# Products of two rotation-table steps on ScalarE, and the tables' steps in other chunks of the FFN

## The chip, the core and the metric

The kernel runs on one core of a Trainium2 chip. A core has TensorE for matrix products, VectorE, ScalarE and GpSimd for the rest, and SyncE, which here only issues DMAs. The metric is the device time of one execution in microseconds, lower is better. One execution is also profiled; its trace gives every instruction's start and duration, counted from the span's start.

## The reference, cut to what matters

Two layers, each with three sub-layers: an FFN, a mixer of four token mixers side by side, a second FFN. The change touches what is done during the first FFN of each layer for the fourth mixer, the S5.

```
for l in range(DEPTH):
    y = _swiglu(u, ffn_w13[l, 0], ffn_w2[l, 0])      # silu(u @ w1) * (u @ w3), then @ w2
    x = _layer_norm(ALPHA * x + 0.5 * gate[:, 0] * y, ...)
    y = _hybrid_mixer(u, ...)                        # A, B, C and S5
    ...
# S5: a diagonal complex recurrence over 256 positions
mag = jnp.exp(lr * dt)
a_re, a_im = mag * jnp.cos(li * dt), mag * jnp.sin(li * dt)
# s[t] = a * s[t - 1] + bu[t], y = Re(C s) + D u
```

All is float32. The sizes: 256 tokens, model width 1024, FFN width 2816.

## The kernel before, in words

**The recurrence by rotation.** The kernel turns the inputs `bu` by the angle of each position, so that a real scan with the factor `rho` is left, and turns the result back. For that it needs cos and sin of n times the angle for n = 0 to 128: `cos_t` and `sin_t`, 128 partitions x 8 tiles x 129. They are built by doubling in seven steps, k = 0 to 6, with m = `TABLE_STEPS[k]` = 1, 2, 4 up to 64. Step k knows the entries 1 to m and makes m + 1 to 2m with the addition theorem: four products into four pieces of `rot_flat` (`t4[0]` to `t4[3]`), a difference and a sum. In `table_ops` VectorE makes each product in one instruction over all 8 tiles (L1245), then the difference (L1248) and the sum (L1251). The semaphore `rot_step` counts all six; a step's sums wait for 4 counts beyond the step before. `TABLE_AT` says behind which chunk of the first FFN which steps are made; SyncE waits once for all of them (chunk 9 of layer 0, as it loads new data into `rot_flat`), and VectorE before the mixer.

**An FFN chunk.** The FFN's 2816 columns are done in 11 chunks of 256, each of two tiles of 128 (ft = 0, 1). The products run in fp32r, and each operand is split into a high and a low part, so that three matmuls make one product of nearly full precision. Per chunk, the engines do, each in the written order:
- TensorE (`ffn_chunk`, L547 to L549): 96 matmuls of the input weights, tile 0 and then tile 1; in some chunks then a sum or a spread of modulation (L521, L530: `spread_gate`); then 24 matmuls with the output weights (L573, L576, L577), the first half with `h` of tile 0, the second with that of tile 1 (in the last chunk all of token tile 0 comes first).
- ScalarE: silu of tile 0 (L1658), the high part of the next chunk's input weights, tile 0 (`w_in_hi`, L1665), the same for tile 1, a gate copy in some chunks, and then `w_out_high` (L1673), two instructions. These wait until TensorE has done the whole chunk, as there is one pair of `w_out_hi` buffers.
- VectorE: the low part of the output weights, twice (`w_out_low`, L1057); then for each tile `ffn_tile`: silu times the linear half (L1041), the high part (L1044) and the low part (L1046) of `h` into `h_parts`; behind it the low part of the next chunk's input weights (L1052). Then, if the chunk stands in `ADA`, one block of the adaLN projection (`ada_block`, L974 or L977 and seven of L980, 128x512 each). Behind these come the small S5 jobs at their chunk: `residual`, `s5_angles`, `s5_poles`, the table steps, `s5_inverse`, `s5_gains`, and `c_blocks` (L1227) and `b_blocks`, which prepare the matrices C and B of the S5.
- SyncE issues the loads of the next chunk's weights, each when the ring's buffer is free, and the block of the adaLN projection.

In layer 0 every chunk of the first FFN has an `ADA` block but the last (which has one in two halves), in layer 1 chunks 0 to 4 and 7 to 9. Chunks 7 and 8 of layer 0 and 3 and 4 of layer 1 spread a gate. The queues are written out by hand; the order in each engine's queue is that of the code.

Of the kernel before, what the change touches and what calls it, by code (L numbers as in the profile page):

```python
# [22 lines left out]
ACT = mybir.ActivationFunctionType  # L23
# [68 lines left out]
TABLE_STEPS = (1, 2, 4, 8, 16, 32, 64)  # L92
ROT_STEPS = 6 * len(TABLE_STEPS)
# [7 lines left out]
def trunk(nc, x, c, ada_w, ada_b, ln_g, ln_b, ffn_w13, ffn_w2, w_in, w_out, sinks, w_uq, w_iq,  # L101
# [3 lines left out]
    with ctx:  # L105
        def sb(name, shape, dt=F32):
            offset[name] = (nc.sbuf_base + 31) // 32 * 32
            return ctx.enter_context(nc.sbuf_tensor(name, shape, dt))
# [7 lines left out]
        def sem(name):  # L116
            if name not in sems:
                sems[name] = ctx.enter_context(nc.semaphore(name))
            return sems[name]
# [28 lines left out]
        cos_t = sb("cos_t", [P, 8, HT + 1])  # L148
        sin_t = sb("sin_t", [P, 8, HT + 1])
# [38 lines left out]
        rot_flat = sb("rot_flat", [P, 8 * T])  # L188
# [42 lines left out]
        def heads(ap):  # L231
            return ap.rearrange("p (t h) -> p t h", t=2)
# [25 lines left out]
        def ff_group(f, c):  # L258

            return (0, G_FFN2)[f] + c  # L260
# [643 lines left out]
        def _(v):  # L904
# [155 lines left out]
            def ffn_chunk(l, f, c):  # L1060

                slot = ff_group(f, c) % 2
                tile = ff_tile(l, f, c)
                for ft in range(2):
                    w_out_low(slot, ft, tile + ft)
                for ft in range(2):
                    ffn_tile(ft, tile)
                    if c != CHUNKS - 1:
                        w_in_low(1 - slot, ft, tile + (2 + ft))
                if c in ADA[l, f]:  # L1070
                    n = ADA[l, f][c]
                    ada_block(n, ada_w_sb, "ada_loaded", n + 1 if n < 10 else n - 1)
# [45 lines left out]
            def residual(l, s, k):  # L1118

                n, tt = l * 3 + s, k // 2  # L1120
                if k % 2 == 0:
                    v.wait_ge(sem("ln_bc_loaded"), (n + 1) * 32)
                    v.wait_ge(sem("xn_act"), n * 2 + (tt + 1))
                    if tt == 1:
                        v.wait_ge(sem("xn_dve"), n + 1)
                    v.tensor_tensor(x_sb[:, tt, :], xn[:, tt, :], ln_bc[:, 0, :], ALU.mult).then_inc(sem("x_step"), 1)
                else:
                    v.wait_ge(sem("x_step"), n * 2 + (tt + 1))
                    v.tensor_tensor(x_sb[:, tt, :], x_sb[:, tt, :], ln_bc[:, 1, :], ALU.add).then_inc(sem("x_ready"), 1)
# [19 lines left out]
            for l in range(DEPTH):  # L1149
# [4 lines left out]
                def s5(ins):  # L1154

                    ins.then_inc(sem("s5_step"), 1)
                    step[0] += 1
                    v.wait_ge(sem("s5_step"), l * STEPS + step[0])
# [17 lines left out]
                def s5_poles():  # L1176

                    v.wait_ge(sem("sin_ready"), l + 1)
                    s5(v.tensor_tensor(S5["sh2"], S5["sinh"], S5["sinh"], ALU.mult))
                    s5(v.tensor_scalar(S5["cos"], S5["sh2"], -2.0, 1.0, ALU.mult, ALU.add))  # L1180

                    v.tensor_copy(cos_t[:, :, 1:2], S5["cos"].unsqueeze(2)).then_inc(sem("rot_start"), 1)
                    v.tensor_copy(sin_t[:, :, 1:2], S5["sin"].unsqueeze(2)).then_inc(sem("rot_start"), 1)
                    s5(v.tensor_tensor(S5["a_re"], S5["rho"], S5["cos"], ALU.mult))
                    s5(v.tensor_tensor(S5["a_im"], S5["rho"], S5["sin"], ALU.mult))
                    s5(v.tensor_scalar(S5["am1"], S5["a_re"], 1.0, None, ALU.subtract))
# [10 lines left out]
                def s5_gains():  # L1197

                    s5(v.tensor_tensor(S5["k1"], S5["k1"], S5["k2"], ALU.add))
                    s5(v.tensor_tensor(S5["k_re"], S5["k1"], S5["rden"], ALU.mult))  # L1200
                    s5(v.tensor_tensor(S5["k3"], S5["a_im"], lr, ALU.mult))
                    s5(v.tensor_tensor(S5["k4"], S5["am1"], li, ALU.mult))
                    s5(v.tensor_tensor(S5["k3"], S5["k3"], S5["k4"], ALU.subtract))
                    s5(v.tensor_tensor(S5["k_im"], S5["k3"], S5["rden"], ALU.mult))
# [18 lines left out]
                def c_blocks():  # L1223

                    v.wait_ge(sem("params_loaded"), (l + 1) * 16 * PARAM_DMAS)
                    for k, sign in ((0, 1.0), (1, -1.0)):
                        v.scalar_tensor_tensor(c_blk[:, k, :, :], c_blk[:, k, :, :], sign,  # L1227
                                               block_mask[:, :].unsqueeze(1).to_broadcast([P, 2, P]), ALU.mult, ALU.mult
                                               ).then_inc(sem("c_blk_ready"), 1)

                def table_ops(k, ops):
# [8 lines left out]
                    for op in ops:  # L1240
# [8 lines left out]
                        else:  # L1249
                            v.wait_ge(sem("rot_step"), at + 4)  # L1250
                            v.tensor_tensor(sin_t[:, :, hi], t4[2], t4[3], ALU.add).then_inc(sem("rot_step"), 1)  # L1251

                TABLE_AT = {3: ((0, range(6)), (1, range(6))), 4: ((2, range(6)), (3, range(6))), 5: ((4, range(6)),),
                            6: ((5, range(6)),), 7: ((6, range(0, 3)),), 8: ((6, range(3, 6)),)}

                for c in range(CHUNKS - 1):
                    ffn_chunk(l, 0, c)
                    if l and c < 4:
                        residual(l - 1, 2, c)
                    if c == 3:  # L1260
                        s5_poles()
                    for k, ops in TABLE_AT.get(c, ()):
                        table_ops(k, ops)
                    if c == 4:
                        s5_inverse()
                    if c == 5:
                        s5_gains()
                    if c == 9:
                        c_blocks()
                        b_blocks()  # L1270
                    if c == 0 and l == 0:
                        bias_constants()
                    if c == 1:
                        v.wait_ge(sem("prm_turned"), l + 1)
                        v.tensor_copy(prm[:, :], PS[:, 7, 0:ROWS]).then_inc(sem("prm_ready"), 1)
                    if c == 2:
                        s5_angles()
# [106 lines left out]
                for tt, cols in ((0, slice(0, P)), (1, slice(P, 384))):  # L1384
                    v.wait_ge(sem("z_read"), l * NZ + 1 + ZN[("t0", "t1")[tt]])
                    for h in range(H):
                        w = tokv[:, tt, 192 + h:193 + h]
                        src = work[0][:, h, cols]
# [97 lines left out]
                for h in range(H):  # L1486
                    g = PS[:, 6 + h // 2, (h % 2) * T:(h % 2 + 1) * T]
                    v.scalar_tensor_tensor(work[0][:, h, 0:T], g, heads(rcol)[:, 0, h:h + 1], mask_c[:, :], ALU.add, ALU.add)
                    ins = v.scalar_tensor_tensor(work[0][:, h, T:384], g[:, P:T], heads(rcol)[:, 1, h:h + 1], mask_c[:, 0:P],
                                                 ALU.add, ALU.add)  # L1490
# [130 lines left out]
        def _(a):  # L1621
# [26 lines left out]
            def copy_gate(n):  # L1648
# [3 lines left out]
                a.activation(gate_bc[s % 2][:, hf * 512:(hf + 1) * 512], PS[:, 7, :], ACT.Copy, scale=1.0 if s % 3 == 1 else 0.5  # L1652
                             ).then_inc(sem("gate_ready"), 1)

            def silu_tile(ft, tile):
                a.wait_ge(sem("ag_ready"), tile + (ft + 3))
                a.wait_ge(sem("h_done"), tile + (ft + 1))
                a.activation(silu_ring[:, ft, :], PS[:, 4 + ft, 0:T], ACT.Silu).then_inc(sem("silu_ready"), 1)  # L1658
# [16 lines left out]
            def ffn_chunk(l, f, c):  # L1675

                last = c == CHUNKS - 1
                slot = ff_group(f, c) % 2
                tile = ff_tile(l, f, c)
                for ft in range(2):  # L1680
                    silu_tile(ft, tile)
                    if not last:
                        if ft == 0:
                            a.wait_ge(sem(f"w_in_loaded{1 - slot}"), in_loads(l, ff_group(f, c + 1)))
                        w_in_high(1 - slot, ft, tile + (2 + ft))
                if not last:
                    if c - 1 in ADA[l, f] and gate_of(ADA[l, f][c - 1]) is not None:
                        copy_gate(ADA[l, f][c - 1])
                    w_out_high(l, f, c + 1)
                elif c - 1 in ADA[l, f] and gate_of(ADA[l, f][c - 1]) is not None:  # L1690
                    copy_gate(ADA[l, f][c - 1])
# [4 lines left out]
            for l in range(DEPTH):  # L1696
                w_out_high(l, 0, 0)
                for c in range(CHUNKS):
                    ffn_chunk(l, 0, c)
                    if c == 1:  # L1700
                        a.wait_ge(sem("prm_ready"), l + 1)
                        a.activation(S5["dt"], log_dt[:, :], ACT.Exp).then_inc(sem("dt_ready"), 1)
                    if c == 2:
                        a.wait_ge(sem("lrdt_ready"), l + 1)
                        a.activation(S5["rho"], S5["lrdt"], ACT.Exp)
                        a.wait_ge(sem("angle_ready"), l + 1)
                        a.activation(S5["sin"], S5["r0"], ACT.Sin)
                        a.activation(S5["sinh"], S5["r0"], ACT.Sin, scale=0.5).then_inc(sem("sin_ready"), 1)
# [245 lines left out]
```

## Time and profile before

| | |
|---|---|
| median of 3 runs | 1121.68 us (1121.27 to 1126.46) |
| profiled execution | 1123.7 us, its span 1121.4 us |
| TensorE busy | 1054.8 us, 94% |
| VectorE busy | 903.8 us, 81% |
| ScalarE busy | 422.4 us, 38% |
| GpSimd busy | 38.9 us, 3% |
| TensorE's granted clock, mean | 0.971 of full speed |
| HBM, mean | 223 GB/s |

The busy shares are means over the whole span. Durations of neighbouring instructions on one engine overlap by a little, so the time that one costs in a row is the distance of two starts. The granted clock is the share of full speed that TensorE got.

### The profile page before, as it was taken

The page shows a single profiled execution, that of the slowest core. Times are in us where ns is not written, and L with a number is a line of the kernel's source. Part 1 is how long each engine was busy: PE and PEld are TensorE (multiplying, and loading weights), DVE is VectorE, ACT ScalarE, POOL GpSimd, SP SyncE. Part 2 cuts the span into 40 slices and gives each one's busy share as a digit, 9 for nine tenths or more (in the row PEclk, how much of TensorE's full clock was granted, in tenths as well). Part 3 has the DMA queues.
Part 4 walks back from the last instruction along what each step waited for, and adds up shares of the span by engine and source line. Part 5 has one row for each costly group of instructions (what it writes and reads, how often), then busy time and mean ns, then how long its engine had stood idle before and what let it go on. Part 6 is the DMA issues. An engine that isn't in the chain of part 4 may idle for free.

```text
span 1121.4 us, 16954 instructions
## 1 busy us (share of the span) xinstructions
PE 1054.8 (94%) x6865; PEld 929.0 (83%) x6865; DVE 903.8 (81%) x1499; ACT 422.4 (38%) x566; POOL 38.9 (3%) x56
## 2 busy tenths in 40 slices
PE   1899999989999899999999999999999989999994
PEld 1899989977865799999989989998787569999994
DVE  6798999989975798988877998798797578755555
ACT  0445334312462334333333443332236333333331
POOL 1000000003000100000000000000300010000000
PEclk9999999989999899999979999999999989999998
DMA  9899998972351588898955886887225156564540
GB/s 367 277 327 310 345 306 301 313 217 75 95 188 38 188 296 288 308 325 286 338 189 190 302 303 196 287 317 199 78 89 203 55 188 233 181 220 148 196 151 37
DMA packets 184504, 250.82 MB, mean 224 GB/s; under 512 B 25372, under 2 KB 133216, under 8 KB 183404
## 3 DMA queue, kind: packets, MB, share of 16 engines
q1 hardware_dynamic: 184428, 249.76, 65.2%
q8 instruction: 54, 0.88, 0.3%
q14 instruction: 22, 0.18, 0.0%
HBM read 248.69 MB, written 1.05 MB: 223 GB/s over the span
## 4 chain that ended last, share of the span: by engine, by line
PE 79%; DVE 14%; issue 2%; ACT 2%; DMA 2%; SPq 0%; POOL 0%; POOLq 0%; DVEq 0%; ACTq 0%
PE PS L547 13%; PE PS L548 13%; PE PS L549 13%; PE PS L654 8%; PE PS L573 6%; PE PS L577 6%; PE PS L576 6%; PE PS L879 2%; DVE w_in_lo L1052 2%; PE PS L661 2%; PE PS L739 2%; DVE acc L980 2%; DMA xn<-in_ada_w_dram 2%; DVE qk_tanh L980 1%; DVE w_out_lo L1057 1%
## 5 line engine op out<-in xcount | busy, mean ns | idle before, releaser
L547 PE MATMUL PS<-u_hi,w_in_hi 128*128 128x256 f32 x1408 | 399.8, 284 | 7.2 <-DVE u_lo L1011 4.4
L549 PE MATMUL PS<-u_hi,w_in_lo 128*128 128x256 f32 x1408 | 400.1, 284 | 0.0
L548 PE MATMUL PS<-u_lo,w_in_hi 128*128 128x256 f32 x1408 | 399.3, 284 | 0.0
L547 PEld LDWEIGHTS PS<-u_hi,w_in_hi 128*128 128x128 f32 x1408 | 270.6, 192 | 10.2 <-issue 5.5
L548 PEld LDWEIGHTS PS<-u_lo,w_in_hi 128*128 128x128 f32 x1408 | 269.3, 191 | 1.6
L549 PEld LDWEIGHTS PS<-u_hi,w_in_lo 128*128 128x128 f32 x1408 | 268.7, 191 | 0.0
L1052 DVE TENSOR_TENSOR w_in_lo<-w_in_ring,w_in_hi 128x2048 fp32r<-128x2048 f32 x88 | 201.5, 2289 | 31.8 <-ACT w_in_hi L1665 31.6
L1665 ACT ACTIVATE w_in_hi<-w_in_ring 128x2048 fp32r<-128x2048 f32 x88 | 168.1, 1914 | 1.3 <-DMA w_in_ring<-in_ffn_w_dram 1.3
L573 PE MATMUL PS<-w_out_hi,h_parts 128*128 128x512 f32 x352 | 144.8, 411 | 7.1 <-DVE h_parts L1046 7.1
L1658 ACT ACTIVATE arena<-PS 128x256 f32<-128x256 f32 x88 | 33.9, 385 | 301.3 <-PE PS L549 301.2
L1673 ACT ACTIVATE w_out_hi<-w_out_ring 128x1024 fp32r<-128x1024 f32 x88 | 88.6, 1055 | 146.4 <-PE PS L577 146.4
L577 PE MATMUL PS<-w_out_hi,h_parts 128*128 128x512 f32 x352 | 139.0, 395 | 0.0
L576 PE MATMUL PS<-w_out_lo,h_parts 128*128 128x512 f32 x352 | 138.6, 394 | 0.0
L1057 DVE TENSOR_TENSOR w_out_lo<-w_out_ring,w_out_hi 128x1024 fp32r<-128x1024 f32 x88 | 103.7, 1219 | 16.3 <-ACT w_out_hi L1673 16.0
L654 PE MATMUL PS<-uT,w_in_ring 128*128 128x256 f32 (+1 forms) x416 | 95.4, 386 | 3.6 <-ACT uT L1634 2.5
L1041 DVE TENSOR_TENSOR arena<-arena,PS 128x256 f32<-128x256 f32 x88 | 36.8, 419 | 75.6 <-ACT arena L1658 75.5
L654 PEld LDWEIGHTS PS<-uT,w_in_ring 128*128 128x128 f32 (+1 forms) x416 | 77.9, 190 | 18.8 <-issue 4.5
L573 PEld LDWEIGHTS PS<-w_out_hi,h_parts 128*128 128x128 f32 x352 | 66.5, 189 | 27.8 <-issue 15.0
L980 DVE SCALAR_TENSOR_TENSOR acc<-arena,cs,acc 128x512 f32<-128x512 f32 x112 | 84.2, 752 | 4.0
L576 PEld LDWEIGHTS PS<-w_out_lo,h_parts 128*128 128x128 f32 x352 | 66.5, 189 | 15.8 <-issue 2.6
L577 PEld LDWEIGHTS PS<-w_out_hi,h_parts 128*128 128x128 f32 x352 | 66.4, 189 | 15.8
L1910 POOL TENSOR_TENSOR rstd<-var_eps,neg_half 128x1 f32<-128x1 f32 x12 | 10.5, 875 | 888.0 <-DVE var_eps L1106 888.0
(302 smaller groups left out, 1068.6 us busy)
## 6 DMA issues: line engine op xcount, KB each, us to landing
w_in_ring<-in_ffn_w_dram SPq DMA_DIRECT2D x88, 1024.0 KB, 7.7
arena<-in_ada_w_dram SPq DMA_DIRECT2D x30, 2048.0 KB, 8.5
w_out_ring<-in_ffn_w_dram SPq DMA_DIRECT2D x44, 1024.0 KB, 6.6
w_in_ring<-in_w_in_dram SPq DMA_DIRECT2D x6, 1024.0 KB, 6.8
w_in_ring<-in_w_in_dram SPq DMA_DIRECT2D x10, 512.0 KB, 4.9
w_out_ring<-in_w_out_dram SPq DMA_DIRECT2D x4, 1024.0 KB, 9.7
w_in_ring<-in_w_in_dram SPq DMA_DIRECT2D x2, 2048.0 KB, 9.4
w_in_ring<-in_w_out_dram SPq DMA_DIRECT2D x4, 1024.0 KB, 6.2
```

The lines of the kernel that those rows point to most:

```text
L547: pe.matmul(y, hi, u_hi[:, kt, :], start=(i == 0), stop=False)
L548: pe.matmul(y, hi, u_lo[:, kt, :], start=False, stop=False)
L549: mm = pe.matmul(y, lo[:, kt, half, :], u_hi[:, kt, :], start=False, stop=(i == KT - 1))
L573: mm = pe.matmul(y, h_hi, w_out_hi[ft][:, cols], start=(first and ft == 0), stop=False)
L576: pe.matmul(y, h_hi, w_out_lo[slot][:, ft, cols], start=False, stop=False)
L577: mm = pe.matmul(y, h_lo, w_out_hi[ft][:, cols], start=False, stop=(last and ft == 1))
L654: mm = pe.matmul(o[0:w, :], w_in_ring[(G_MIX + m) % 2][:, kt, c0:c0 + w], uT[:, kt, :], start=(kt == 0), stop=(kt == KT - 1))
L980: v.scalar_tensor_tensor(acc[:, :], part(buf, t), cs[:, t:t + 1], acc[:, :], ALU.mult, ALU.add).then_inc(sem("acc_step"), 1)
L1052: v.tensor_tensor(w_in_tile(w_in_lo, slot, ft), w_in_tile(w_in_ring, slot, ft), w_in_hi[ft][:, :, :, :].bitcast(F32), ALU.subtract).then_i ...
L1057: v.tensor_tensor(w_out_lo[slot][:, ft, :], w_out_ring[slot][:, ft, :], w_out_hi[ft][:, :].bitcast(F32), ALU.subtract).then_inc(sem("w_out ...
L1665: a.activation(w_in_hi[ft][:, :, :, :], w_in_tile(w_in_ring, slot, ft), ACT.Copy).then_inc(sem("w_in_high"), 1)
L1673: a.activation(w_out_hi[ft][:, :], w_out_ring[slot][:, ft, :], ACT.Copy).then_inc(sem("w_out_high"), 1)
```

## The change

Three edits. First, in steps 5 and 6 of the tables ScalarE makes the products: a new function `table_products` with 8 instructions for each of the four products, one for each tile, as ScalarE takes its factor as one value for each partition; 32 a step. It stands behind ScalarE's chunk 6 and 7 in layer 0, and 7 and 8 in layer 1. VectorE makes only the ops 4 and 5 (difference and sum) of these steps, behind the chunks of the same numbers. Second, `TABLE_AT` now differs by layer: in layer 0 steps 0 to 4 stay where they were; in layer 1 steps 0 to 3 come behind chunk 5 and step 4 behind chunk 6. Third, `c_blocks` comes behind chunk 8 in layer 0, and stays behind chunk 9 in layer 1.

```
-                TABLE_AT = {3: ((0, range(6)), (1, range(6))), 4: ((2, range(6)), (3, range(6))), 5: ((4, range(6)),),
-                            6: ((5, range(6)),), 7: ((6, range(0, 3)),), 8: ((6, range(3, 6)),)}
+                steps = lambda *ks: tuple((k, range(6)) for k in ks)
+                TABLE_AT = ({3: steps(0, 1), 4: steps(2, 3), 5: steps(4), 6: ((5, (4, 5)),), 7: ((6, (4, 5)),)},
+                            {5: steps(0, 1, 2, 3), 6: steps(4), 7: ((5, (4, 5)),), 8: ((6, (4, 5)),)})[l]
...
+                    if c == 8 + l:
+                        c_blocks()
                     if c == 9:
-                        c_blocks()
                         b_blocks()
...
+            def table_products(l, k):
+
+                m = TABLE_STEPS[k]
+                t4 = [rot_flat[:, 512 * q:512 * q + 8 * m].rearrange("p (i n) -> p i n", i=8) for q in range(4)]
+                a.wait_ge(sem("rot_step"), l * ROT_STEPS + 6 * k)
+                for q, (src, by) in enumerate(((cos_t, cos_t), (sin_t, sin_t), (sin_t, cos_t), (cos_t, sin_t))):
+                    for i in range(8):
+                        ins = a.activation(t4[q][:, i, :], src[:, i, 1:1 + m], ACT.Copy, scale=by[:, i, m:m + 1])
+                    ins.then_inc(sem("rot_step"), 1)
...
                 for c in range(CHUNKS):
                     ffn_chunk(l, 0, c)
+                    if c in (6 + l, 7 + l):
+                        table_products(l, c - l - 1)
```

## Rows read from the trace of the kernel before

**Rows 1.** Waits of TensorE, 105 to 240 us: total, times, longest.

```profile
PE PS L573 <- DVE h_parts L1046: 4.4, 6, 2.5
```

**Rows 2.** Timeline of TensorE, layer 0: start us, us, engine, line, tiles.

```profile
162.65 0.28 PE L547 MATMUL PS<-u_hi,w_in_hi 128*128 128x256 f32 x1
...
174.00 1.02 PE L530 MATMUL PS<-acc,ones 128*128 128x512 f32 x2
...
233.21 0.47 PE L573 MATMUL PS<-w_out_hi,h_parts 128*128 128x512 f32 x1 [2.51 <-DVE h_parts L1046]
```

**Rows 3.** Timeline of ScalarE, layer 1, `w_out_hi` of chunks 4 to 7.

```profile
655.72 2.01 ACT L1673 ACTIVATE w_out_hi<-w_out_ring 128x1024 fp32r<-128x1024 f32 x2 [4.13 <-PE PS L577]
...
674.58 2.02 ACT L1673 ACTIVATE w_out_hi<-w_out_ring 128x1024 fp32r<-128x1024 f32 x2 [4.88 <-PE PS L577]
...
692.51 2.02 ACT L1673 ACTIVATE w_out_hi<-w_out_ring 128x1024 fp32r<-128x1024 f32 x2 [4.44 <-PE PS L577]
...
709.41 2.02 ACT L1673 ACTIVATE w_out_hi<-w_out_ring 128x1024 fp32r<-128x1024 f32 x2 [3.41 <-PE PS L577]
```

**Rows 4.** Timeline of ScalarE, layer 0, chunk 7 and the start of chunk 8.

```profile
162.91 2.01 ACT L1673 ACTIVATE w_out_hi<-w_out_ring 128x1024 fp32r<-128x1024 f32 x2 [3.90 <-PE PS L577]
168.53 0.39 ACT L1658 ACTIVATE arena<-PS 128x256 f32<-128x256 f32 x1 [3.61 <-PE PS L549]
...
180.67 2.02 ACT L1673 ACTIVATE w_out_hi<-w_out_ring 128x1024 fp32r<-128x1024 f32 x2 [3.79 <-PE PS L577]
```

**Rows 5.** Timeline of VectorE, layer 0, chunks 6 to 10.

```profile
169.41 0.43 DVE L1248 TENSOR_TENSOR cos_t<-rot_flat 128x256 f32<-128x256 f32 x1
...
170.08 2.35 DVE L1057 TENSOR_TENSOR w_out_lo<-w_out_ring,w_out_hi 128x1024 fp32r<-128x1024 f32 x2
172.36 0.41 DVE L1041 TENSOR_TENSOR arena<-arena,PS 128x256 f32<-128x256 f32 x1
...
175.68 0.41 DVE L1041 TENSOR_TENSOR arena<-arena,PS 128x256 f32<-128x256 f32 x1
...
185.18 0.69 DVE L1245 TENSOR_TENSOR rot_flat<-cos_t 128x512 f32<-128x512 f32 x1
...
203.01 0.69 DVE L1248 TENSOR_TENSOR cos_t<-rot_flat 128x512 f32<-128x512 f32 x1
...
204.22 2.36 DVE L1057 TENSOR_TENSOR w_out_lo<-w_out_ring,w_out_hi 128x1024 fp32r<-128x1024 f32 x2
...
220.05 0.75 DVE L1227 SCALAR_TENSOR_TENSOR c_blk<-c_blk,block_mask 128x256 f32<-128x256 f32 x2
...
231.87 0.41 DVE L1041 TENSOR_TENSOR arena<-arena,PS 128x256 f32<-128x256 f32 x1
```

**Rows 6.** ScalarE: timeline rows, and two groups by shape (busy us, mean ns).

```profile
98.88 0.21 ACT L1707 ACTIVATE s5p<-s5p 128x8 f32<-128x8 f32 x1
99.00 0.19 ACT L1708 ACTIVATE s5p<-s5p 128x8 f32<-128x8 f32 x1
...
309.42 2.88 ACT L1754 ACTIVATE work_flat<-work_flat,small 128x128 f32<-128x128 f32 x8
...
L1754 ACT ACTIVATE work_flat<-work_flat,small 128x256 f32<-128x256 f32 x16 | 6.8, 493 | 0.0
...
L1754 ACT ACTIVATE work_flat<-work_flat,small 128x128 f32<-128x128 f32 x16 | 5.1, 391 | 2.2 <-DVE small L1501 2.1
```

**Rows 7.** Timeline of VectorE, layer 1, chunks 3 to 5.

```profile
663.06 0.17 DVE L1245 TENSOR_TENSOR rot_flat<-cos_t 128x8 f32<-128x8 f32 x1
...
664.52 2.35 DVE L1057 TENSOR_TENSOR w_out_lo<-w_out_ring,w_out_hi 128x1024 fp32r<-128x1024 f32 x2
...
670.11 0.41 DVE L1041 TENSOR_TENSOR arena<-arena,PS 128x256 f32<-128x256 f32 x1
...
688.04 0.41 DVE L1041 TENSOR_TENSOR arena<-arena,PS 128x256 f32<-128x256 f32 x1
```

**Rows 8.** Busy time by window, 232 to 240 us; PEclk is the granted clock.

```profile
232.00:240.00 8.00, 6.53 (x24) 5.04 (x24) 6.54 (x16) 0.00 (x0) 0.56 (x1) 0.79 0.96 199
```

## The prediction, made before the changed kernel was run

> **What bounds the kernel now.** I read the busy shares first (in the table above): TensorE 94%, VectorE 81%, ScalarE 38%. A share is an average, so I looked next at TensorE's waits over the chunks of layer 0's first FFN [rows 1]: 4.4 us in 135 us, all of it for `h_parts`, which VectorE writes. TensorE sets the pace, and VectorE is only just in time. The timelines then give the rhythm of a chunk. I count from T, the chunk's first matmul.
>
> TensorE does the input products until T + 11.35 (162.65 to 174.00 [rows 2]) and then the output products. An undisturbed chunk is 16.90 long (692.51 to 709.41 [rows 3]), so the output products take 5.55, in two halves of 2.78: the first needs `h` of tile 0, the second, due at T + 14.13, that of tile 1. Chunks that also spread a gate take 17.76 (162.91 to 180.67 [rows 4]); there the second half is due at 17.76 - 2.78 = T + 14.98.
>
> ScalarE makes `w_out_hi` at T + 0.26, two instructions in 2.01, and has nothing more to do until the first silu, at T + 5.88 (168.53 [rows 4]).
>
> VectorE runs, in this order: table work, `w_out_low` twice, the multiply of tile 0, `w_in_low`, the multiply of tile 1. In chunk 7 of layer 0 the reader sees 170.08, 172.36 and 175.68 [rows 5]: 2.28 from `w_out_low` to the first multiply (m0), 3.32 from there to the second (m1). TensorE starts on an `h` 1.34 after its multiply (231.87 [rows 5], 233.21 [rows 2]). So VectorE may start `w_out_low` at 14.13 - 1.34 - 3.32 - 2.28 = T + 7.19 before an undisturbed chunk gets longer, and at T + 8.04 in a chunk with a gate. Chunk 7 started it at T + 7.43. There is little to spend.
>
> **Part 1: VectorE gives up eight products in each layer, and waits instead.** In place of four products with two sums, VectorE makes two sums. The sums of step 5 take 0.67 (169.41 to 170.08), those of step 6 take 1.21 (203.01 to 204.22); four products of step 5, of the sums' shape, took about 4 x 0.34 = 1.36 [rows 5]. But the sums wait until ScalarE has made all four groups, 32 instructions, and ScalarE begins these only behind `w_out_hi` of the next chunk. Queued behind the waiting sums on VectorE are the next chunk's `w_out_low` and both multiplies, and TensorE waits for these.
>
> The trace has no ScalarE instruction of 32 or 64 columns with a scale taken from a column. The nearest: `over_sums` (L1754), the same Copy with such a scale from SBUF to SBUF. It takes 391 ns for 128 columns and 493 ns for 256, and four of each end 2.88 us after the first starts [rows 6]. The durations add up to 3.54, so consecutive ones overlap by 0.66/7 = 0.094. The slope is 0.102/128 = 0.80 ns a column. That makes 0.314 for 32 columns and 0.340 for 64, and a step from one to the next of 0.22 and 0.245. I take these. The lower end is the shortest start-to-start step of two small instructions there, 0.12 at 8 columns (98.88 to 99.00 [rows 6]), without such a scale: with 24 and 56 columns more, 0.14 and 0.165.
>
> The products start at T + 0.26 + 2.01 - 0.09 = T + 2.18.
> Step 5: the last ends at 2.18 + 31 x 0.22 + 0.31 = T + 9.31. Sums from T + 9.34, `w_out_low` at T + 10.01, m0 at 12.29, TensorE's output products at 13.63 (due 11.35), m1 at 15.61, second half at 16.95, chunk ends at T + 19.73.
> Step 6: the last ends at 2.18 + 31 x 0.245 + 0.34 = T + 10.12. Sums, `w_out_low` at 11.36, m0 13.64, TensorE at 14.98, m1 16.96, second half at 18.30, end at T + 21.08.
>
> VectorE itself would be ready for step 5's sums at about T + 5.4 (169.41 less 1.36, less 162.65), and for step 6's at 15.61 + 9.50 (175.68 to 185.18 [rows 5]) - 19.73 = T + 5.4, so ScalarE's end decides both. ScalarE's silu comes 3.4 to 4.3 late; with `w_in_hi` behind it, it has caught up by about T + 12, long before VectorE asks at m1.
>
> The price, chunk by chunk (the sums of layer 0 fall at the start of chunks 7 and 8, both with a gate; those of layer 1 at the start of 8 and 9, both undisturbed, as their `ADA` entries hold no gate):
> layer 0: 19.73 - 17.76 = +1.97, and 21.08 - 17.76 = +3.32;
> layer 1: 19.73 - 16.90 = +2.83, and 21.08 - 16.90 = +4.18.
> Together +12.30. The lateness does not run on: after chunk 8 VectorE comes to `w_out_low` of chunk 9 at 16.96 + 9.50 - 21.08 + 0.67 (the c blocks) = T + 6.05.
>
> **Part 2: `c_blocks` of layer 0 moves from chunk 9 to chunk 8.** Two instructions, 0.75 [rows 5], 0.67 when the overlap with the next is taken off. At its old place it lies in an unbroken run of VectorE before the last chunk's multiplies, for which TensorE waits 2.51 [rows 2]: -0.67. At its new place there is room (T + 6.05 against 8.04): 0. In layer 1 it stays.
>
> **Part 3: layer 1's steps 0 to 4 go to chunks 5 and 6.** Chunks 4 and 5 of layer 1 are long: 655.72 to 674.58 is 18.86, and 17.93 follow to 692.51 [rows 3]. Steps 0 and 1 took 1.46 (663.06 to 664.52 [rows 7]). Without them m1 of chunk 4 (670.11) comes at 668.65 and TensorE can use it at 669.99, T + 14.53 < 14.98: chunk 4 takes 17.76, -1.10. Without steps 2 and 3 as well, another 1.46 at least, m1 of chunk 5 (688.04) could come at 685.12, T + 11.9 of a chunk that starts at 673.22; TensorE uses it by T + 13.3 < 14.13: 16.90, -1.03. At the new places VectorE is free: chunks 5 and 6 of layer 1 have no ada block (8 x about 0.76). Should that cover be missing, the 3.3 us of steps 0 to 3 would show in full. DMA issues don't move, and SyncE's one wait on the tables (`rot_step`, chunk 9) is met earlier.
>
> **Sum:** +12.30 - 0.67 - 2.13 = +9.5 us. The profiled execution took 1123.7 (span 1121.4 and 2.3 around it), so it would be 1133.2. The median of the runs shown is 1121.68, 2.0 below that execution; I predict it at 1131.2.
>
> **Rules of the Trainium skill weighed.** The trace has four products on VectorE in about 1.4 us [rows 5] and, by the step worked out above, 32 instructions in 7 us on ScalarE. The Trainium skill (ScalarE: Activation LUTs, section Rules for kernel authors) says to use VectorE and not ScalarE for multiplications. The trace agrees; by that rule the +12.30 would not be there, and the sum would be -2.8. The same table budgets about 0.3 us for each ACTIVATE and 0.83 ns an element. The trace contradicts that as a step: [rows 6] have eight in 2.88 us, where that budget makes 3.7.
>
> **Rivals.**
> *A, ScalarE in time, no change.* The small products run at the lower end's step, and ScalarE's idle stretch of 3.6 us before the first silu nearly holds them. Step 5 then ends at 6.71 and costs +0.22 in layer 1, nothing in layer 0; step 6 ends at 7.55, `w_out_low` 8.79, second half 15.73, +0.75 and +1.60. Sum 2.57 - 2.80 = -0.2: 1121.4. It decides at a step of 0.131, below which step 5 costs nothing. For it: that row of 8 columns. Against it: the closer form has the scale operand, and its fixed part (391 - 102 - 94 = 0.195 us) is paid by each.
> *B, faster.* If the products ended before VectorE was ready at T + 5.4, only parts 2 and 3 would remain, and step 5's relief: 1121.68 - 2.8 = 1118.9. This needs a step of 0.10, under any row. VectorE's high share speaks for it; that TensorE waits so little [rows 1] caps what relief can give.
> *C, slower still: the clock falls.* After the wait of 2.51 at the end of layer 0 the granted clock was 0.79 over 8 us [rows 8]: 1.7 us of full speed lost, part of it at 1.2 GHz. The new waits are 2.3 us (step 5) and 3.6 us (step 6, less in layer 0, where the gate fills 0.86). 0.5 us before the second half absorbs some; a fall costs 1.2. One or two are likely and stand against my slightly high step; all four make +4.8: 1136.
> *D, no overlap at all.* If each small instruction cost what its duration says, without the overlap of 0.094, each of the four stages would end 31 x 0.094 = 2.9 later: +11.7, 1142.9. The row of eight speaks against it. By the Trainium skill's budget (above) it would be 3.3 each, near 1144.6.
>
> **Chances.** Forecast 0.64; A, or something between A and the forecast, 0.18 (of which half under 1127.3); B 0.02; C 0.13; D 0.03. The likeliest case by itself runs from 1127.5 (a step of 0.19) to 1134 (two falls of the clock). Range 1123 to 1137: it leaves out most of A's own point, B and D. A measurement of this kernel can tell about 0.5%, 5.6 us: faster than 1116.1 0.02; within 0.14; slower than 1127.3 0.84.
>
> **What would show it.** In layer 0's chunks 7 and 8: silu 0 at about T + 9.3 and 10.1 in place of 5.88; VectorE idle about 4 and 5 us before its two sums, released by ScalarE; chunk lengths 19.7 and 21.1. In layer 1: chunks 4 and 5 at 17.8 and 16.9, chunks 8 and 9 at 19.7 and 21.1. The last chunk's wait of 2.51 unchanged, with everything behind 0.67 nearer to the chunk's start. Wrong would be: a step of ScalarE's products under 0.15 or near 0.31; a TensorE wait in chunks 7 to 9 that isn't for `h_parts`; or chunks 5 and 6 of layer 1 that grow.

## The result, and the profile after

| | before | after |
|---|---|---|
| median | 1124.07 us (1121.27 to 1128.65, 4 runs) | 1137.59 us (1135.97 to 1139.21, 4 runs) |
| profiled execution, span | 1123.7, 1121.4 | 1138.59, 1136.3 |
| TensorE, VectorE, ScalarE busy | 1054.8, 903.8, 422.4 us | 1059.3, 896.1, 450.8 us |
| mean granted clock | 0.971 | 0.961 |

The ratio is 1.0116, with a 95% interval of 1.0093 to 1.0139: 10 to 16 us slower. The forecast was slower by 9.5 us, in a range that ended at 1137.0; the direction was right, the size too small. In absolute time the median lies 6.4 us above the forecast of 1131.2; 2.4 of them are the kernel before itself, whose median is 1124.07 here and was 1121.68 in the runs that the forecast stood on, and 4.0 are the change. Two later controls of the same kernel gave 1.0152 and 1.0134. The ratios leave out two slow executions of about 2107.6 us, nearly twice the rest: one of `vector_products` and one of the kernel before beside it.

First the waits of the kernel after, in the stretches that hold the two stages of each layer. Columns: waiting engine, tile, line, releaser; total, times, longest.

```profile
ACT w_out_hi L1685 <- PE PS L577: 16.3, 3, 6.7
DVE cos_t L1248 <- ACT rot_flat L1664: 8.5, 2, 4.7
PEld PS L573 <- issue: 6.6, 4, 3.3
PE PS L573 <- DVE h_parts L1046: 4.2, 4, 2.5
...
ACT w_out_hi L1685 <- PE PS L577: 23.5, 4, 9.5
ACT arena L1670 <- PE PS L549: 18.1, 6, 3.6
DVE cos_t L1248 <- ACT rot_flat L1664: 10.1, 2, 6.0
DVE arena L1041 <- ACT arena L1670: 5.7, 3, 2.6
PEld PS L573 <- issue: 5.7, 2, 3.5
PE PS L573 <- DVE h_parts L1046: 5.3, 2, 3.3
```

The group above the dots is 160 to 205 us (layer 0), the one below 700 to 780 us (layer 1). There is a new line in each: VectorE's `cos_t` waits for ScalarE's `rot_flat`, twice in each layer. TensorE's wait for `h_parts` follows from it: 4.2 us in 45 us, where the kernel before had 4.4 in 135 [rows 1], and in the same 45 us only this:

```profile
PE PS L573 <- DVE h_parts L1046: 0.2, 1, 0.2
```

The timeline of ScalarE after, layer 0, chunk 7 (T = 161.08, the chunk's first matmul) and the start of chunk 8:

```profile
161.34 2.02 ACT L1685 ACTIVATE w_out_hi<-w_out_ring 128x1024 fp32r<-128x1024 f32 x2 [3.88 <-PE PS L577]
163.26 1.79 ACT L1664 ACTIVATE rot_flat<-cos_t 128x32 f32<-128x32 f32 x8
164.95 1.79 ACT L1664 ACTIVATE rot_flat<-sin_t 128x32 f32<-128x32 f32 x8
166.65 1.80 ACT L1664 ACTIVATE rot_flat<-sin_t,cos_t 128x32 f32<-128x32 f32 x8
168.35 1.79 ACT L1664 ACTIVATE rot_flat<-cos_t,sin_t 128x32 f32<-128x32 f32 x8
170.06 0.36 ACT L1670 ACTIVATE arena<-PS 128x256 f32<-128x256 f32 x1
...
180.99 2.01 ACT L1685 ACTIVATE w_out_hi<-w_out_ring 128x1024 fp32r<-128x1024 f32 x2 [5.68 <-PE PS L577]
182.90 2.02 ACT L1664 ACTIVATE rot_flat<-cos_t 128x64 f32<-128x64 f32 x8
184.81 2.02 ACT L1664 ACTIVATE rot_flat<-sin_t 128x64 f32<-128x64 f32 x8
```

And VectorE's, the same chunk:

```profile
170.25 0.42 DVE L1248 TENSOR_TENSOR cos_t<-rot_flat 128x256 f32<-128x256 f32 x1 [3.79 <-ACT rot_flat L1664]
170.59 0.42 DVE L1251 TENSOR_TENSOR sin_t<-rot_flat 128x256 f32<-128x256 f32 x1
170.93 2.35 DVE L1057 TENSOR_TENSOR w_out_lo<-w_out_ring,w_out_hi 128x1024 fp32r<-128x1024 f32 x2
173.20 0.41 DVE L1041 TENSOR_TENSOR arena<-arena,PS 128x256 f32<-128x256 f32 x1
...
176.52 0.41 DVE L1041 TENSOR_TENSOR arena<-arena,PS 128x256 f32<-128x256 f32 x1
```

Eight products of step 5 start 1.70 after the eight before them, 0.212 apiece; those of step 6 1.915, 0.239 apiece. In the order of the forecast: silu 0 at T + 8.98 (5.88 before, [rows 4]), `w_out_low` at T + 9.85 (7.43), the multiplies at 12.12 and 15.44. The forecast had 10.01, 12.29 and 15.61.

The chunk lengths, as distances of the chunks' first matmuls in the timelines (in us):

| | layer 0: 7, 8 | layer 1: 4, 5 | layer 1: 8, 9 |
|---|---|---|---|
| before | 17.76, 17.75 | 18.85, 17.93 | 16.90, 16.90 |
| forecast | 19.73, 21.08 | 17.76, 16.90 | 19.73, 21.08 |
| after | 19.65, 21.03 | 17.75, 16.89 | 20.67, 23.33 |

Four of the six are within 0.1 us of the forecast. Layer 1's chunks 8 and 9 are 1.0 and 2.3 longer than their twins in layer 0, although VectorE's and ScalarE's rows in them stand at the same distances from T. The timeline of TensorE shows where (chunk 9 of layer 1, output products):

```profile
765.25 0.76 PE L573 MATMUL PS<-w_out_hi,h_parts 128*128 128x512 f32 x1 [3.35 <-DVE h_parts L1046]
765.82 0.63 PE L576 MATMUL PS<-w_out_lo,h_parts 128*128 128x512 f32 x1
766.24 0.63 PE L577 MATMUL PS<-w_out_hi,h_parts 128*128 128x512 f32 x1
...
771.62 0.40 PE L573 MATMUL PS<-w_out_hi,h_parts 128*128 128x512 f32 x1
771.85 0.40 PE L576 MATMUL PS<-w_out_lo,h_parts 128*128 128x512 f32 x1
```

After a wait of 3.35 the matmuls stand 0.43 apart; from 771.4 on they stand 0.23 apart again. The busy time by window gives the granted clock (third number from the end) there and in chunk 8:

```profile
744.10:747.50 3.40, 3.40 (x10) 2.61 (x9) 3.33 (x5) 0.00 (x0) 0.00 (x0) 0.50 0.78 239
764.60:771.40 6.80, 6.15 (x15) 4.82 (x16) 6.66 (x9) 0.00 (x0) 0.00 (x0) 0.50 0.62 185
```

The clock stood at 0.50, that is 1.2 GHz, for 3.4 us in chunk 8 and 6.8 us in chunk 9. In layer 0's chunks 7 and 8 of this profile it stayed at 1.00.

The four chunks together are 15.4 us longer than before, chunks 4 and 5 of layer 1 are 2.1 shorter, and the last chunk of layer 0 begins its output products 12.42 after its start in place of 13.09: the 0.67 of `c_blocks`. The span grew by 14.9, 1.6 more than the six chunks make. That rest is the sum of the other stretches. The largest are the one from layer 0's last chunk through its mixer, 165.93 for 162.50 although it holds the 0.67 won, and the stretch before chunk 1, 1.7 shorter.

### The profile page after: what moved, and what is told of

Its sections match the earlier page's. It is cut to its first block, busy times and chain, and to the rows that moved or that the text cites. A ratio compares the mean times of both kernels' runs of the same rounds, so it can differ in the third digit from the quotient of the medians.

```text
span 1136.3 us, 17064 instructions
## 1 busy us (share of the span) xinstructions
PE 1059.3 (93%) x6865; PEld 929.3 (82%) x6865; DVE 896.1 (79%) x1483; ACT 450.8 (40%) x694; POOL 38.9 (3%) x56
## 4 chain that ended last, share of the span: by engine, by line
PE 74%; DVE 14%; ACT 5%; issue 3%; DMA 2%; SPq 1%; POOL 0%; POOLq 0%; DVEq 0%; ACTq 0%
PE PS L547 12%; PE PS L548 12%; PE PS L549 12%; PE PS L654 8%; PE PS L573 6%; PE PS L577 6%; PE PS L576 6%; ACT rot_flat L1664 2%; PE PS L879 2%; PE PS L661 2%; DMA w_in_ring<-in_ffn_w_dram 2%; PE PS L739 2%; DVE w_in_lo L1052 2%; DVE acc L980 2%; DVE w_out_lo L1057 2%
## 5 line engine op out<-in xcount | busy, mean ns | idle before, releaser
L1057 DVE TENSOR_TENSOR w_out_lo<-w_out_ring,w_out_hi 128x1024 fp32r<-128x1024 f32 x88 | 103.6, 1219 | 17.1 <-ACT w_out_hi L1685 16.9
L654 PE MATMUL PS<-uT,w_in_ring 128*128 128x256 f32 (+1 forms) x416 | 98.3, 394 | 3.6 <-ACT uT L1636 2.6
```

What stands on the lines that cost most here:

```text
L654: mm = pe.matmul(o[0:w, :], w_in_ring[(G_MIX + m) % 2][:, kt, c0:c0 + w], uT[:, kt, :], start=(kt == 0), stop=(kt == KT - 1))
L1057: v.tensor_tensor(w_out_lo[slot][:, ft, :], w_out_ring[slot][:, ft, :], w_out_hi[ft][:, :].bitcast(F32), ALU.subtract).then_inc(sem("w_out ...
```

## The experiments

All ratios are to the kernel before, measured beside it, with the 95% interval. Lengths of chunks are read from each kernel's profile.

### The three edits apart

The other two edits without the first:

```
+                TABLE_AT = ({3: steps(0, 1), 4: steps(2, 3), 5: steps(4), 6: steps(5), 7: ((6, range(0, 3)),), 8: ((6, range(3, 6)),)},
+                            {5: steps(0, 1, 2, 3), 6: steps(4, 5), 7: ((6, range(0, 3)),), 8: ((6, range(3, 6)),)})[l]
...
-                    if c in (6 + l, 7 + l):
-                        table_products(l, c - l - 1)
```

> The changed kernel with all products back on VectorE (step 5 whole behind chunk 6, step 6 in two parts behind chunks 7 and 8); the other two edits stay (layer 1's steps 0 to 4 in chunks 5 and 6, its step 5 in chunk 6, c_blocks of layer 0 in chunk 8). Theory of the four stages: all that was lost goes, and the two gains are left, chunks 4 and 5 of layer 1 at 17.8 and 16.9 us and 0.7 off the last chunk of layer 0: 2.8 us under the kernel before, within 0.3% of it. Rival, that the placement of the steps or the moved c_blocks is what lengthens the kernel (the mixer of layer 0 took 3 us longer after the change): then it stays 3 us or more above before.

Measured: 0.9984 (0.9968 to 1.0000), median 1121.65. The four chunks are 17.75, 17.75, 16.90 and 16.90, layer 1's chunks 4 and 5 are 17.76 and 16.89. All of the loss is gone with the first edit, and the gains are there.

The first edit without the others (`TABLE_AT` of before for steps 0 to 4 in both layers, `c_blocks` behind chunk 9 in both):

> Only the first edit: ScalarE makes the products of steps 5 and 6, VectorE the sums; layer 1's steps 0 to 4 and c_blocks stay where they were before. Four stages: chunks 7 and 8 of layer 0 at 19.65 and 21.03, chunks 8 and 9 of layer 1 at the same or longer where the clock falls; chunks 4 and 5 of layer 1 at 18.85 and 17.93. 12.0 us above before without a fall of the clock, about 15 with them. Rival (the other two edits matter): it comes out at the changed kernel's time of about 13 or below.

Measured: 1.0122 (1.0099 to 1.0145). Chunks 7 and 8 of layer 0: 19.63, 21.05; 4 and 5 of layer 1: 18.83, 17.95; 8 and 9: 20.66, 21.87. The chunks are as expected; chunk 9 is shorter than in the changed kernel (23.33), as the low clock lasted 3.4 us in it and not 6.8. The chunks add up to 13.9 us above before, and 1.0122 is 13.7. The whole should be 2.8 us slower than the control beside it (1.0152) and came out faster; the two intervals overlap, so the times do not tell, and the 2.8 us rest on the chunks of the profiles.

### What the products cost: their number, and their place

One instruction a product, in place of eight (the factor is a constant, so the tables hold other numbers):

```
-                    for i in range(8):
-                        ins = a.activation(t4[q][:, i, :], src[:, i, 1:1 + m], ACT.Copy, scale=by[:, i, m:m + 1])
+                    ins = a.activation(t4[q], src[:, :, 1:1 + m], ACT.Copy, scale=0.7)
```

> The changed kernel with one ScalarE instruction for each of the four products, over all 8 tiles with the constant factor 0.7 in place of the tables' entries (so the tables hold other numbers). Same elements, 4 instructions a step in place of 32. If the cost is the instructions' fixed part: the products end at T + 3.5 (step 5) and T + 4.4 (step 6), before VectorE is ready at about 5.4; chunks 7 and 8 of layer 0 at 17.76, 8 and 9 of layer 1 at 16.90; time 1 to 3 us under before. Rival, that it is the elements or the crossing between the engines: the chunks stay above 19.

Measured: 0.9976 (0.9959 to 0.9993). The chunks are 17.75, 17.75, 16.90, 16.90. The same elements in four instructions cost nothing. In its timeline one product of 256 columns takes 418 ns, where eight of 32 columns took 1.79 us. So the cost is the fixed part, paid 32 times; neither the elements nor the crossing from ScalarE to VectorE costs. The edit also replaces the factor read from a column by a constant; how much of each small instruction's fixed part belongs to that operand is not separated here.

The same 32 instructions, in front of `w_out_hi`:

```
+                    if f == 0 and c in (6 + l, 7 + l):
+                        table_products(l, c - l - 1)
                     w_out_high(l, f, c + 1)
```

> The changed kernel with one thing moved: ScalarE makes the 32 products before w_out_hi of the next chunk, in the 3.8 us in which it waits for TensorE, and not behind it. They start at about T + 13.5 and end at 20.3 and 21.6, 3.4 and 4.7 into the next chunk; w_out_hi comes late by these, but VectorE is ready only at 5.4. Placement theory: the four chunks are back at 17.76, 17.76, 16.90 and 16.90, time 2 to 3 us under before (ratio 0.997 to 0.999). Rival, that 32 instructions in front of anything in the chunk cost: at least one of the four chunks is over 18 us.

Measured: 0.9976 (0.9961 to 0.9991), chunks 17.76, 17.75, 16.90, 16.90. ScalarE's timeline, chunk 7 of layer 0 into chunk 8:

```profile
173.41 1.91 ACT L1677 ACTIVATE w_in_hi<-w_in_ring 128x2048 fp32r<-128x2048 f32 x1
175.22 0.59 ACT L1654 ACTIVATE gate_bc<-PS 128x512 f32<-128x512 f32 x1
175.69 2.02 ACT L1664 ACTIVATE rot_flat<-cos_t 128x64 f32<-128x64 f32 x8
...
181.45 2.01 ACT L1664 ACTIVATE rot_flat<-cos_t,sin_t 128x64 f32<-128x64 f32 x8
183.36 2.00 ACT L1685 ACTIVATE w_out_hi<-w_out_ring 128x1024 fp32r<-128x1024 f32 x2
185.26 0.37 ACT L1670 ACTIVATE arena<-PS 128x256 f32<-128x256 f32 x1
```

The 7.7 us of work are the same; they now begin in the stretch in which ScalarE had waited for TensorE, and silu 0 follows `w_out_hi` at once, 0.05 later than before. TensorE's waits for `h_parts` over 105 to 215 us, before layer 0's last chunk, are 1.0 us, as before (1.1). The chunks are those of the kernel with all products on VectorE: at this place the products neither cost nor win anything, and the 2.7 us under before (0.9976) are the 2.8 of the other two edits.

### VectorE's wait or ScalarE's lateness

Layer 1 only: ScalarE's products behind its chunks 6 and 8, VectorE's sums behind 7 and 9.

```
+                            {5: steps(0, 1, 2, 3), 6: steps(4), 7: ((5, (4, 5)),), 9: ((6, (4, 5)),)})[l]
...
+                    if l == 1 and c in (6, 8):
+                        table_products(l, c // 2 + 2)
```

> Layer 1 only (layer 0 has its products on VectorE): ScalarE's products behind its chunks 6 and 8, VectorE's sums behind chunks 7 and 9, so VectorE never waits for them, but ScalarE's silu still comes late. If only VectorE's wait costs: chunks 7 and 9 of layer 1 at 16.90. If ScalarE's late silu costs too: VectorE waits for silu 0 at T + 9.0 and 9.8 and then for w_in_hi, so the second multiply comes at about 13.4 and 14.2 in place of 12.0: chunk 7 at 17.5, chunk 9 at 18.4. Chunk 8 at 16.90 in both.

Measured, in one profiled execution: chunk 7 17.58, chunk 8 16.90, chunk 9 18.45. Of the 2.75 and 4.1 that a stage costs there, 0.7 and 1.6 are left when VectorE does not wait for the products. VectorE then waits for silu instead:

```profile
716.35 0.42 DVE L1041 TENSOR_TENSOR arena<-arena,PS 128x256 f32<-128x256 f32 x1 [5.65 <-ACT arena L1670]
...
718.16 2.29 DVE L1052 TENSOR_TENSOR w_in_lo<-w_in_ring,w_in_hi 128x2048 fp32r<-128x2048 f32 x1 [0.60 <-ACT w_in_hi L1677]
720.37 0.41 DVE L1041 TENSOR_TENSOR arena<-arena,PS 128x256 f32<-128x256 f32 x1
```

Most of the cost is the wait on the sums; the late silu, behind the same instructions, is the rest that comes to light when that wait is gone. One cost moved on: with the sums of step 6 behind chunk 9, beside `c_blocks` and `b_blocks`, the last chunk of layer 1 begins its output products 12.50 after its start, where the changed kernel has 11.34.

### The clock

The changed kernel with matmuls of constants in TensorE's waits (one, three, three and five of them in the four chunks), and the control beside it:

```
+                for _ in range({(0, 0, 7): 1, (0, 0, 8): 3, (1, 0, 8): 3, (1, 0, 9): 5}.get((l, f, c), 0)):
+                    pe.matmul(PS[:, 6, 0:384], ones[:, :], dist[:, :], start=True, stop=True)
```

> The changed kernel, with idle matmuls of 0.65 us each (constants, into a free bank) between TensorE's input and output products: one in chunk 7 and three in chunk 8 of layer 0, three in chunk 8 and five in chunk 9 of layer 1, so that TensorE works where it waited. Clock theory: the four chunks are 19.65, 21.03, 19.65, 21.03 and no granted clock of half speed stands in them; 2 to 4 us under the control. Rival, the extra of layer 1 is another wait: the chunks stay at 20.7 and 23.3, time as the control.

> Control: the changed kernel unaltered, on the same chip as the others. 1.2% above before (1.0093 to 1.0139 measured). The chunk lengths of layer 0 and layer 1 without a fall of the clock are again 19.65 and 21.03; where the clock falls differs from run to run.

Measured: filled 1.0111 (1.0087 to 1.0134), control 1.0152 (1.0127 to 1.0177). The chunks of the filled kernel are 19.65, 21.03, 19.65 and 21.05, those of the control 19.65, 22.05, 20.65 and 23.21. Chunk 9 of layer 1 in the filled kernel, TensorE, with the granted clock of 740 to 771 us under it:

```profile
759.18 3.39 PE L553 MATMUL PS<-dist,ones 128*128 128x384 f32 x10
762.68 0.47 PE L575 MATMUL PS<-w_out_hi,h_parts 128*128 128x512 f32 x1
762.99 0.39 PE L578 MATMUL PS<-w_out_lo,h_parts 128*128 128x512 f32 x1
763.22 0.39 PE L579 MATMUL PS<-w_out_hi,h_parts 128*128 128x512 f32 x1
```

```profile
740.00:771.00 31.00, 30.27 (x178) 24.87 (x177) 25.40 (x34) 17.61 (x42) 0.00 (x0) 1.00 0.85 272
```

TensorE has more to do and is done sooner: its matmuls stand 0.23 apart, the clock stays at 1.00, and layer 1's chunks become the twins of layer 0's. The extra of 1.0 and 2.3 us was the clock. All six executions of the filled kernel (1133.57 to 1138.21) lie under all four of the control (1139.35 to 1142.15).

The same pair once more:

> waits_filled once more, on the chip of the control beside it. With the waits filled, the four chunks are 19.65, 21.03, 19.65, 21.05 and nothing else is left of the change but the gains: +9.3 us, ratio 1.0083. It came out at 1.0111 (1.0087 to 1.0134); if that was scatter it comes out lower, if a second mechanism adds 3 us it stays.

> The changed kernel unaltered, for the comparison with the filled waits on one chip. It came out at 1.0116 and 1.0152. Clock theory: 3 to 5 us above the filled kernel again, with falls in chunk 8 or 9 of layer 1 in its profile.

Measured: filled 1.0102 (1.0080 to 1.0124), control 1.0134 (1.0111 to 1.0156); chunks 19.64, 21.04, 19.63, 21.04 against 19.65, 22.03, 20.67, 23.32. In the two pairs the filled kernel is 4.6 and 3.6 us faster by the ratios, though the intervals of each pair overlap a little. Both filled results lie 2 to 3 us above the 9.3 (1.0083) that the chunks add up to; 1.0083 is just outside the first interval and just inside the second.

One step alone on ScalarE, in both layers behind chunk 6 (step 5) or 7 (step 6):

> ScalarE makes the products of step 5 alone, in both layers behind its chunk 6; step 6 is on VectorE in two parts as before; the other two edits stay. One stage in each layer: chunk 7 at 19.65 in both (17.76 and 16.90 without), +1.9 and +2.75, less the gains of 2.8: +1.8 us, ratio 1.0016. TensorE's waits are about 2 us and then 0.5. Clock theory, that the extra hangs on the longer waits of step 6: no fall in these chunks. If falls come at these waits too: +3 to +5.

> ScalarE makes the products of step 6 alone, in both layers behind its chunk 7; step 5 is whole on VectorE in chunk 6; the other two edits stay. Chunk 8 at 21.03 in both layers if the clock holds, +3.3 and +4.1, less 2.8: +4.6 us, ratio 1.0041. The waits are about 2.7 and 3.5 us; clock theory: a fall in at least one of the two chunks, which are then 22 to 23.3 long, and +6 to +8 us.

Measured: step 5 alone 1.0034 (1.0018 to 1.0049), chunk 7 19.63 and 19.64, no fall of the clock in them. The chunks are as forecast, but the whole is 3.8 us above before, where they add up to 1.8, and 1.0016 is outside the interval: here too it is 2 us more than the chunks explain, in a kernel without a fall in its stages. Step 6 alone 1.0077 (1.0053 to 1.0102), chunk 8 22.05 and 23.30: 1.0 and 2.3 above 21.03, a fall in each. That is 8.7 us, where the chunks add up to 7.9. Here the longer waits of step 6 (2.50 and 3.35 us) are followed by a fall in both layers, and the shorter ones of step 5 (1.09 and 1.94) in neither. That is no rule: in layer 1 of the changed kernel step 5's wait of the same length (1.95) is followed by a fall in all three profiles (20.65 to 20.67), and in layer 0 step 6's is in two of three (21.03, 22.05, 22.03).

### Where the last 2 to 3 us are

> One more profile of the kernel with filled waits. If the open 2 to 3 us are scatter outside the chunks: the four chunks are 19.65, 21.03, 19.65, 21.05 again, and a span above 1131 shows in the stretches from a last chunk to the next FFN (163.0, 31.0 and 158.3 us in the first two profiles).

> As the first look: the four chunks fixed, and the difference to the first profiles in the stretches between the FFNs, by the granted clock there.

> A third look at the kernel with filled waits: the four chunks fixed again, and a longer span, if there is one, in the stretches between the FFNs.

> The same look at the kernel with all products on VectorE: its chunks 17.75, 17.75, 16.90 and 16.90 again; its span (1120.4 in the first profile, executions of 1116.9 to 1122.7) moves with the same stretches.

Measured, one execution each: spans 1133.4, 1131.8 and 1129.5 for the filled kernel. The four chunks are 19.63 to 19.65 and 21.02 to 21.05 in all five profiles of it. The stretch from the last chunk of layer 0 to the second FFN was 162.98, 163.07, 165.96, 163.91 and 161.64 (spans 1131.3, 1130.9, 1133.4, 1131.8, 1129.5); it explains most of the spread. The kernel with its products on VectorE has it too: 162.86 and 165.43, at spans of 1120.4 and 1120.3. The five filled spans have a mean of 1131.4, 10.0 above the span before (1121.4) and 11.1 above these two; the stages make 12.1, and 9.3 with the gains. So in the profiles the sum closes to about 1 us. The span before is one profile, though: another execution of that kernel, beside these four, had a span of 1123.5, and the filled mean is 7.9 above that. Why the timed executions stand 2 to 3 us higher than the sum is not settled, and step 5 alone shows the same 2 us without a fall in its stages: the longest profiled execution of the filled kernel took 1135.72 (span 1133.4), and eight of its twelve timed ones took that or more. Another cost of the stages outside the four chunks is not excluded.

### A version that uses the room

The products in front of `w_out_hi`, and in layer 0 `s5_inverse` behind chunk 7 and `s5_gains` behind chunk 8, where VectorE now has time:

```
-                    if c == 4:
+                    if c == 7 - 3 * l:
                         s5_inverse()
-                    if c == 5:
+                    if c == 8 - 3 * l:
                         s5_gains()
```

> As products_before_w_out, and in layer 0 the room that VectorE gets in chunks 7 and 8 is used: s5_inverse goes from chunk 4 to 7 and s5_gains from 5 to 8. Chunks 5 and 6 of layer 0, 17.94 and 17.38 before, fall to 16.9; chunk 4 stays at 17.4, chunks 7 and 8 at 17.76. 4 to 5 us under before (ratio 0.996). If VectorE's lateness in chunks 5 and 6 has another cause, it is the time of products_before_w_out.

Measured: 0.9964 (0.9949 to 0.9978), median 1120.26. Chunks 5 and 6 of layer 0 are 16.90 and 16.90, chunks 4, 7 and 8 are 17.41, 17.76 and 17.75. It is faster than the kernel before and than the changed one. Against the version with the products in front alone (0.9976) the intervals overlap; there the gain of 1.5 us rests on chunks 5 and 6 of the profile. Whether the same two moves would pay with the products left on VectorE was not tested.

## Why the prediction fell short

**What bounds, and how much VectorE may be late: right.** In the four stages VectorE starts `w_out_low` at T + 9.85 and T + 11.25; less the due times of T + 7.19 and T + 8.04 that makes 2.66, 1.81, 4.06 and 3.21, and the chunks grew by 2.75, 1.89, 4.15 and 3.28 where the clock held. Where VectorE did not wait for the products (`sums_a_chunk_later`), the late silu set the length instead, as its expectation had it.

**Part 1, the stages: right, mechanism and size.** +12.30 was forecast and 12.07 measured where the clock held (the filled kernel). The step between ScalarE's instructions was 0.212 and 0.239 for the 0.22 and 0.245 taken from [rows 6]. Rivals A (a step of 0.14) and D (no overlap) are out by these steps, and B by the chunks. By the Trainium skill (ScalarE: Activation LUTs, section What ACT_TABLE_LOAD costs), an ACTIVATE takes 186 ns and 0.833 ns an element, with 93 ns more for each pointer operand, and neighbours overlap by 93 ns. Worked out from that, an estimate for 32 and 64 columns with one such operand is a step of 0.213 and 0.239 us; the trace's 0.212 and 0.239 agree.

**Part 2, `c_blocks`: right,** -0.67: layer 0's last chunk begins its output products 12.42 after its start in place of 13.09.

**Part 3, layer 1's steps: right,** -1.10 and -1.04 for -1.10 and -1.03.

**The step that failed is the clock's term in the sum: it was put at nothing, and it measured 3.3 to 4.3 us.** The forecast knew the row (0.79 after a wait of 2.51, [rows 8]) and the waits to come (2.3 and 3.6 us), said that one or two falls were likely, and then set them off against a "slightly high step". That step made the four stages 0.2 us too long in all. In the three profiles of the changed kernel two, three and three of the four stages had a fall, and the falls cost 3.3, 4.2 and 4.3 us. The price of 1.2 for one fall held in the chunks that grew by 1.0, but chunk 9 of layer 1, where the low clock lasted 6.8 us and covered 15 of the 24 output matmuls of the first profile, grew by 2.3. The measured stages and gains (9.3) with the falls make 12.6, 13.5 and 13.6, and 1.0116, 1.0152 and 1.0134 are 13.0, 17.1 and 15.1 us. Rival C, at a chance of 0.13, had the right mechanism; its size, falls in all four stages for +4.8, was never reached.

What is left, 0.4, 3.6 and 1.5 us, stays open, as told above. The median passed the top of the range, 1137, by 0.6 us, less than the 2.4 by which the kernel before itself stood higher; on the base that the forecast used, the change of 13.5 would have ended at 1135.2, between the likeliest case and rival C's 1136. So the miss of the range is in part chance, and the failed term is not.

## What to carry to other kernels

Work that is moved to an idle engine is priced by its place in that engine's queue: in four stages of 32 instructions each, these products cost 12.1 us, and the falls of the clock on top, behind `w_out_hi`, and nothing in front of it, since there they filled a wait instead of starting one. An instruction has a fixed part (on ScalarE here 0.19 of the 0.212 us from one product of 32 columns to the next, by the steps of 32 and 64 columns), so a product that another engine makes in one instruction and this one in eight is to be priced by its count. And where an edit makes TensorE wait in a stretch that it bounds, the wait is not the whole price: a price for the matmuls behind it at half the clock, here 0.8 to 2.3 us a fall, belongs in the sum itself.

## What the runs showed of the hardware

Five idle matmuls (ten records, 3.4 us) in a wait of TensorE made the chunk 2.2 us shorter: the granted clock stayed at 1.00 instead of 0.50, and the output products stood 0.23 apart in place of 0.43. Over the whole kernel the twelve idle matmuls in four waits were worth 3.6 to 4.6 us by the ratios. A wait of 1.95 us was followed by a fall in chunk 8 of layer 1 of the changed kernel, and one of 1.94 was not in chunk 7 of layer 1 with step 5 alone on ScalarE. The unfilled wait of step 6 in layer 1 was followed by one in all five profiles that have it: the chunk took 23.33, 23.21, 23.32, 21.87 and 23.30 in place of 21.05.
